# Rotating queries and keys in the projection, and making attention's first maxima key chunk by key chunk

## The reference, cut to what matters

```python
def apply_rope(x, cos, sin):
    half = x.shape[-1] // 2
    x1, x2 = x[..., :half], x[..., half:]
    return jnp.concatenate([x1 * cos - x2 * sin, x1 * sin + x2 * cos], axis=-1)

def diff_attend(q, k, v, lam):
    s = jnp.einsum('bqhmd,bkhmd->bhmqk', q, k) * (DA_QK ** -0.5)
    p = jax.nn.softmax(s, axis=-1)
    w = p[:, :, 0] - lam * p[:, :, 1]
    return jnp.einsum('bhqk,bkhv->bqhv', w, v)
```

## Time and profile before

| | us |
|---|---|
| median of 3 runs | 7244.72 (7240.84 to 7279.03) |
| the profiled execution | 7235.89 |
| its span | 7234.0 |
| PE busy | 5861.2 (81%) |
| DVE busy | 3119.6 (43%) |
| ACT busy | 1715.9 (24%) |
| POOL busy | 2013.9 (28%) |
| projections, by the trace | about 150 to 1250 and 3700 to 4960 |
| attentions start, by the trace | 2515.9 and 6082.9 |

### The profile page before, as it was taken

The page is one execution under the profiler, slowest core; times in us unless marked ns, Lnnn a source line. Parts: engine busy times, 40 slices in busy tenths (PEclk is TensorE's granted clock), DMA queues, the critical chain, the costliest instruction groups (busy, mean ns, idle before and its releaser), DMA issues. The chain is left out here.

```text
span 7234.0 us, 78073 instructions
## 1 busy us (share of the span) xinstructions
PE 5861.2 (81%) x27236; PEld 3103.1 (43%) x27272; DVE 3119.6 (43%) x5057; ACT 1715.9 (24%) x4089; POOL 2013.9 (28%) x1396
## 2 busy tenths in 40 slices
PE   4999999812688699998989999996218886999989
PEld 1444444411566533333434444443116664333334
DVE  0222222268566565551122333333875666555412
ACT  1111111100233324443011211211003332344421
POOL 0000000012333348887000000000223332688830
PEclk7999999855899889998999999997559997999989
DMA  7111111044322110001421111112433222000022
GB/s 257 49 45 45 47 46 44 31 134 130 107 79 79 54 34 7 7 5 41 192 91 49 45 47 46 47 40 63 126 117 104 79 86 64 1 7 7 4 83 92
DMA packets 294466, 475.52 MB, mean 66 GB/s; under 512 B 112612, under 2 KB 165172, under 8 KB 287268
## 3 DMA queue, kind: packets, MB, share of 16 engines
q1 hardware_dynamic: 262500, 383.00, 15.7%
q10 hardware_dynamic: 25632, 55.62, 2.1%
q0 software_dynamic: 6048, 33.11, 1.3%
HBM read 313.82 MB, written 157.51 MB: 65 GB/s over the span
## 5 line engine op out<-in xcount | busy, mean ns | idle before, releaser
L456 PE MATMUL psum<-group_W,projection_hT 128*128 128x512 f32 (+2 forms) x5040 | 2024.8, 559 | 52.5 <-DVE projection_hT L548 52.5
L456 PEld LDWEIGHTS psum<-group_W,projection_hT 128*128 128x128 f32 x5040 | 967.6, 193 | 1062.6 <-issue 1020.0
L1965 POOL TENSOR_TENSOR attention_SA<-attention_SA,attention_PT 128x1024 f32<-128x1024 f32 x512 | 1193.3, 2350 | 123.5 <-ACT attention_PT L2107 78.9
L2023 DVE TENSOR_REDUCE attention_mxp<-psum 128x1 f32<-128x512 f32 (+1 forms) x1016 | 653.6, 686 | 646.2 <-PE psum L2144 645.5
L2107 ACT ACTIVATE attention_PT<-psum 128x512 f32<-128x512 f32 (+1 forms) x1168 | 630.4, 592 | 888.1 <-PE psum L2193 859.4
L565 DVE TENSOR_SCALAR projection_e<-projection_e 128x256 f32<-128x256 f32 (+1 forms) x180 | 57.5, 319 | 1499.6 <-ACT projection_e L512 1499.6
L2144 PE MATMUL psum<-attention_QK 32*128 32x512 f32 (+1 forms) x2592 | 678.8, 642 | 10.3 <-DVE attention_mxp L2012 6.7
L2187 PE MATMUL psum<-attention_QK 32*128 32x512 f32 x2336 | 676.2, 656 | 0.0
L2205 PE MATMUL psum<-attention_PT,attention_va 128*64 128x512 f32 x2336 | 642.7, 630 | 0.0
L505 ACT ACTIVATE projection_ut<-psum 128x512 f32<-128x512 f32 (+1 forms) x360 | 149.9, 427 | 1696.8 <-PE psum L456 1696.8
L2318 PE MATMUL psum<-output_W,output_yT 128*128 128x512 f32 x1088 | 477.1, 597 | 20.4 <-DMA output_W<-in_w_out 20.4
(11 more groups left out here) (329 smaller groups left out, 7039.1 us busy)
## 6 DMA issues: line engine op xcount, KB each, us to landing
u<-projection_ut SPq DMA_DIRECT2D x252, 256.0 KB, 2.0
states_x<-xbc SPq DMA_DIRECT2D x108, 384.0 KB, 4.2
mixing_hg<-u SPq DMA_DIRECT2D x36, 1024.0 KB, 5.0
modulation_wm<-in_w_mod SPq DMA_DIRECT2D x12, 2048.0 KB, 8.7
group_W<-in_w_in SPq DMA_DIRECT2D x8, 2316.0 KB, 33.7
output_y<-y SPq DMA_DIRECT2D x34, 512.0 KB, 4.5
group_W<-in_w_in POOLq DMA_DIRECT2D x6, 2316.0 KB, 27.4
xbc<-projection_ut SPq DMA_DIRECT2D x36, 384.0 KB, 2.3
```

The lines of the kernel that those rows point to most:

```text
L456: ins = nc.tensor.matmul(ps[n % RING][:, 0:w], hT[b][:, q], W[q][:, c0:c0 + w], start=(q == 0), stop=(q == KT - 1))
L1965: G.tensor_tensor(SA[x % 2][:, rs, 0:w], one[:, rs, 0:w], PT[i % PTB][:, rs, 0:w], ALU.add) \
L2023: bk.release(V.tensor_reduce(mxp[x % 2][:, q:q + nn, 2 * pr + j, a], bk[job, j][:, 0:nn * (hi - lo)].rearrange("p (q n) -> p q n", q=nn), ...
```

## The change

The projection rotates the queries and keys itself. For block 3 ACT copies nothing any more; DVE multiplies the bank with the cosines and (half-swapped) with the sines, frees the bank, and writes the sum to `u`. The cosines and sines of the round's two tiles are loaded by SP at the start of each round (24 KB each), ahead of the round's stores. The counts of ACT's copies fall from 9 to 8 a tile.

Attention loads the rotated tiles and PE transposes them at once, into banks 4 and 5 (the prologue uses 0 to 3, 6 and 7); ACT copies as before. SP issues the small constants first, and loads a tile when the buffer's former tile is transposed. ACT makes the small exponential of `lm` ahead of its copies. The prologue's order becomes chunk, query tile, pair. PE turns six tiles (two of the context and the four of the first queries), two more before the first chunk, and ahead of each further chunk the tiles that the chunk after it needs (four, four, two), between the jobs of the maxima.

```diff
@@ projection
-             3: [(OFF["da_q"], 512, 1.0)], 4: [(OFF["da_v"], 256, 1.0)], 5: [(OFF["ss_xbc"], 512, 1.0)],
+             3: [], 4: [(OFF["da_v"], 256, 1.0)], 5: [(OFF["ss_xbc"], 512, 1.0)],
...
                 for r, kind, i in rounds(sp):
                     for b in range(2):
+                        sp.dma_start(rp[b][:].rearrange("p a f -> p (a f)"), k.rope[r * 2 + b]).then_inc(s[f"rope_in{b}"], 16)
+                    for b in range(2):
                         t = r * 2 + b
...
+                            if n == 3:
+                                hold(sp, s["rotated"], r * 2 + (b + 1), s["turns"])
...
                         for n, (c0, w) in enumerate(BLOCKS):
+                            if n == 3:
+                                continue
                             act.wait_ge(s["block_mm"], r * 20 + (b * 10 + n + 1))
...
+                            if n == 3:
+                                lo, w = BLOCKS[n]
+                                four = lambda a: a.rearrange("p (n x f) -> p n x f", x=2, f=16)
+                                cos = rp[b][:, 0].unsqueeze(1).unsqueeze(1).to_broadcast([P, w // 32, 2, 16])
+                                sin = rp[b][:, 1:3].unsqueeze(1).to_broadcast([P, w // 32, 2, 16])
+                                bank = ps[n % RING][:, lo - c0:lo - c0 + w]
+                                dve.wait_ge(s[f"rope_in{b}"], r * 16 + 16)
+                                dve.wait_ge(s["block_mm"], r * 20 + (b * 10 + n + 1))
+                                nc.vector.tensor_tensor(four(ra[:, 0:w]), four(bank), cos, ALU.mult)
+                                nc.vector.tensor_tensor(four(rb[:, 0:w]), skew(bank, 16, [[32, w // 32], [-16, 2], [1, 16]]), sin,
+                                                        ALU.mult).then_inc(s[f"bank_free{n % RING}"], 1)
+                                dve.wait_ge(s[f"bank_free{n % RING}"], r * 4 + (2 * b + 2))
+                                dve.wait_ge(s[f"st{n}"], (r * 2 + b) * 16 + 16)
+                                nc.vector.tensor_tensor(u[:, lo:lo + w], ra[:, 0:w], rb[:, 0:w], ALU.add).then_inc(s["rotated"], 1)
+                                dve.wait_ge(s["rotated"], r * 2 + (b + 1))
...
@@ attention
-    prologue = [(q, a, pr) for q in range(QG) for a in range(5) for pr in range(2)]
+    prologue = [(q, a, pr) for a in range(5) for q in range(QG) for pr in range(2)]
...
-                sp.dma_start(rp[:].rearrange("p t a f -> p t (a f)"), k.rope.rearrange("t p n -> p t n")).then_inc(s["rope_in"], 16)
...
+                for t in range(NT):
+                    b = t % 4
+                    if t >= 4:
+                        sp.wait_ge(s["key_mm"], t - 3)
+                    sp.dma_start(xb[b][:], k.u[t, :, OFF["da_q"]:OFF["da_q"] + 512]).then_inc(s[f"x_in{b}"], 16)
...
-                dve.wait_ge(s["rope_in"], 16)
-                f4 = lambda a: a.rearrange("p (n x f) -> p n x f", x=2, f=16)
-                for t in range(NT):
-                    b = t % 4
-                    dve.wait_ge(s[f"x_in{b}"], 16 * (t // 4 + 1))
-                    cos = rp[:, t, 0].unsqueeze(1).unsqueeze(1).to_broadcast([P, 16, 2, 16])
-                    sin = rp[:, t, 1:3].unsqueeze(1).to_broadcast([P, 16, 2, 16])
-                    V.tensor_tensor(f4(ra[t % 2][:]), f4(xb[b][:]), cos, ALU.mult)
-                    st.then(V.tensor_tensor(f4(rb[t % 2][:]), skew(xb[b][:], 16, [[32, 16], [-16, 2], [1, 16]]), sin, ALU.mult))
-                    if t >= 2:
-                        dve.wait_ge(s["key_mm"], t - 1)
-                    V.tensor_tensor(rot[t % 2][:], ra[t % 2][:], rb[t % 2][:], ALU.add).then_inc(s["rotated"], 1)
...
+                def keys(tiles):
+                    for t in tiles:
+                        pe.wait_ge(s[f"x_in{t % 4}"], 16 * (t // 4 + 1))
+                        if t >= 2:
+                            pe.wait_ge(s["key_copied"], t - 1)
+                        for a in range(4):
+                            ins = nc.tensor.transpose(k.bank[4 + t % 2][:, a * P:(a + 1) * P], xb[t % 4][:, a * P:(a + 1) * P], k.ident[:])
+                        ins.then_inc(s["key_mm"], 1)
...
-                pe.wait_ge(s["key_copied"], NT)
+                made = CT + QG
+                keys(range(made))
                 for n, (q, a, pr) in enumerate(prologue):
+                    if q == 0 and pr == 0:
+                        ahead = min(NT, groups[0][3][a][1] // P + 4)
+                        keys(range(made, ahead))
+                        made = max(made, ahead)
+                        pe.wait_ge(s["key_copied"], max(CT + QG, groups[0][3][a][1] // P))
```

More of the change, by code:

```diff
@@ L362, in projection @@
         small = [k.sb(c, f"small{b}", [P, 8]) for b in range(2)]
+        rp = [k.sb(c, f"rp{b}", [P, 3, 16]) for b in range(2)]
+        ra = k.sb(c, "ra", [P, 512])
+        rb = k.sb(c, "rb", [P, 512])
         G = k.sb(c, "G", [P, KT, 2])
@@ L411, in _ @@
                             if plain[n] and n != 8:
-                                hold(sp, s["copied"], r * 18 + (b * 9 + sum(bool(plain[m]) for m in range(n + 1))), s["turns"])
+                                hold(sp, s["copied"], r * 16 + (b * 8 + sum(bool(plain[m]) for m in range(n + 1))), s["turns"])
+                            if n == 3:
+                                hold(sp, s["rotated"], r * 2 + (b + 1), s["turns"])
                             if n in gated:
@@ L431, in _ @@
                     sp.wait_ge(s[n], 16 * (NT + 1))
+                for b in range(2):
+                    sp.wait_ge(s[f"rope_in{b}"], 8 * NT)
             @block.tensor
@@ L515, in _ @@
                             elif n != 8:
-                                act.wait_ge(s["copied"], r * 18 + (b * 9 + sum(bool(plain[m]) for m in range(n + 1))))
+                                act.wait_ge(s["copied"], r * 16 + (b * 8 + sum(bool(plain[m]) for m in range(n + 1))))
                                 act.sem_inc(s[f"bank_free{n % RING}"], 1)
                             if n == 8:
-                                act.wait_ge(s["copied"], r * 18 + (b * 9 + 8))
+                                act.wait_ge(s["copied"], r * 16 + (b * 8 + 7))
                                 act.sem_inc(s[f"bank_free{n % RING}"], 1)
@@ L2078, in _ @@
                 act.wait_ge(s["memsets"], 1)
+                act.wait_ge(s["lam_dot"], 1)
+                A(lm[:, 0:2], lm[:, 0:2], ACT.Exp).then_inc(s["lam_exp"], 1)
                 for t in range(NT):
                     act.wait_ge(s["key_mm"], t + 1)
-                    A(QK[:, :, t * P:(t + 1) * P], k.bank[t % 4][:].rearrange("p (a n) -> p a n", a=4), ACT.Copy) \
+                    A(QK[:, :, t * P:(t + 1) * P], k.bank[4 + t % 2][:].rearrange("p (a n) -> p a n", a=4), ACT.Copy) \
                         .then_inc(s["key_copied"], 1)
-                act.wait_ge(s["lam_dot"], 1)
-                A(lm[:, 0:2], lm[:, 0:2], ACT.Exp).then_inc(s["lam_exp"], 1)
                 def turned(x):
@@ L2129, in _ @@
                 T = nc.tensor.matmul
-                for t in range(NT):
-                    pe.wait_ge(s["rotated"], t + 1)
-                    if t >= 4:
-                        pe.wait_ge(s["key_copied"], t - 3)
-                    for a in range(4):
-                        ins = nc.tensor.transpose(k.bank[t % 4][:, a * P:(a + 1) * P], rot[t % 2][:, a * P:(a + 1) * P], k.ident[:])
-                    ins.then_inc(s["key_mm"], 1)
+                def keys(tiles):
[6 more added lines that the diff above has]
+                        ins.then_inc(s["key_mm"], 1)
                 rows = lambda r: slice(DQ * r, DQ * r + DQ)
```

15 lines of the change are left out of this document (3 added, 12 removed).

## The result

The changed kernel takes 7192.9 us (median of 5 runs, 7188.0 to 7209.4), the kernel before 7253.5 beside it (5 runs, 7240.8 to 7291.8). The ratio is 0.9892, 95% interval 0.9857 to 0.9928: 52 to 104 us faster. The forecast was 45 us, so faster is right, and the gain, 61 us between the medians and 78 by the ratio, came out above the stated range of 27 to 55. (The time 7192.9 by itself lies between 7186 and 7222, but that range hung on a kernel before at 7244.7, and beside the changed kernel it took 7253.5.) In two further measurements of the same kernel the ratio is 0.9942 and 0.9939. Over all runs made for this study (29 of the changed kernel, 124 of the one before, the experiment *null* included) the mean falls by 45.7 us, interval 33 to 58. The mean over many runs is thus near the forecast.

A forecast was written before the change was run, and what follows sets the result against it. PE bounds the projection, DVE the start of attention. Per layer 28.0 us earlier first product less 5.3 of waits is 22.7, 45.4 in all, projection nothing: 7199 us at the median's level; gain range 27 to 55, 7186 to 7222 once widened.

The forecast's parts named there:

- First tile: Start of attention: the first tile's load, issued at 2516.85 us, lands at 2520.2, with bounds of 2519.5 and 2521.0.
- Pitch of a tile: Start of attention: loaded tiles are transposed one every 1.1 us, with bounds of 0.96 and 1.93, the old pitch.
- First product: Start of attention: after eight turned tiles PE's first product comes 28.0 us earlier than before, bounds 28.9 and 22.2.
- Waits between the chunks: Attention's maxima: DVE waits for PE's inner transposes, 8.6 us a layer at 1.2 GHz, 2.0 at 2.4; 5.3 taken.
- a sign of being wrong: Attention's maxima: DVE idle over 10 us would mean that PE's transposes are dearer than thought.
- First read: Attention's maxima: DVE first reads 2.13 us after PE's first product, an estimated 1.3 at 2.4 GHz.
- rival 3: Attention: the wait moves to the gate's load, POOL late by some 6 us a layer; gain 33, 7212 us, chance 0.04.
- rival 4: Projection: DVE's three instructions at block 3 are exposed, up to 76 us against 45; +31, 7275 us, chance 0.05.
- The sign given for it: Projection: if the forecast is right, PE's busy share stays as before and DVE's idle time falls by 74 us.
- rival 1: Start of attention: loads or a low clock bind, pitch nearer the old one; gain 27 to 36, 7213 us, chance 0.15.
- rival 2: Start of attention: the clock rises and stays, waits of 2.0 us a layer; gain 52, 7193 us, chance 0.10.
- Numbers: Whole kernel: 7190.5 us from the profiled execution, 7199 at the median's level; range widened by 4 us each side.

The follow-up runs named there:

- null: The kernel before timed once more against itself, nothing changed: 7254.5 us (12 runs), ratio 1.001.
- triple: Changed kernel with six more of the rotation's first product on DVE for each tile in the projection: 7211.5 us (10 runs), ratio 0.9928 to the kernel before.
- spread: Changed kernel with PE turning one tile after every second job of the maxima, not blocks before chunks: 7226.8 us (12 runs), ratio 0.9943 to the kernel before.
- again: The changed kernel timed and profiled once more, nothing altered: 7207.9 us (12 runs), ratio 0.9942 to the kernel before.
- proj_only: Changed projection with the attention of before, so queries and keys are rotated twice: 7271.5 us (10 runs), ratio 1.002 to the kernel before.
- fill: Kernel of spread with a bfloat16 product, later overwritten, ahead of each score in the last half of attention: 7566.1 us (6 runs), ratio 1.0402 to the kernel before.

## Why the prediction was right or wrong

**First tile.** The forecast was 4.3 us from the stage's start to its landing; its transposes start at 5.3. The issue is where it was expected, and the landing was slow: 2.6, 3.3 and 4.9 us at least, in the median and at most (2.6, 2.7 and 4.2 before). From issue to use it was 4.4 us for the first tile, against 4.0 before, with the table's load no longer ahead of it. That was the case which the rule of the Trainium skill ("DMA: Bandwidth & Descriptors", Specifications) on transfers under 512 B had priced at 1.2 us better. No such gain is seen; but another load with short rows (`gr`, 256 B a row) stood ahead, so the rule isn't refuted.

**Pitch of a tile.** Forecast 1.1. Seven tiles in 2524.66 - 2517.41 = 7.25 us are 1.04, between PE's 0.96 and the 1.05 of the bytes.

**First product.** Forecast 13.1 us after the stage's start, measured 2525.24 - 2512.14 = 13.10; 28.0 earlier than before, as forecast; over the eight profiled stages of the changed kernel and of *triple* it is 12.8 to 13.4. In the first of them two errors cancel: the landing 1 us late, the pitch and the last transposes (0.66 us, at 2.4 GHz, not 1.12) 0.9 early.

**Waits between the chunks.** Right in place and mechanism, low in size. The forecast for 1.2 GHz was 3.5, 3.5 and 1.6; measured 4.50, 4.50 and 2.68 (11.7 against 8.6). For 2.4 GHz it was 1.0, 1.0 and none; measured 1.38, 1.38 and 2.46, the last of them at a clock that had fallen again, as in the prologue of the earlier trace rows. Over the eight stages the sum is 7.5 us, not the 5.3 taken. *spread* shows that it is all PE's transposes. In three of the eight DVE is idle for over 10 us, which the prediction had named as a sign of being wrong, and for the reason that it gave there: the transposes cost more than thought. The Trainium skill ("TensorE: Matmul & The Clock Gate", HAM oscillation) says that pauses of PE let its clock fall; in three of the eight stages the sum was that of the low clock (11.7 or 11.8), in the others 4.5 to 5.2, so neither level can be counted on. The fall under the column sums came without such a pause: PE was busy, by the profile, for all 2.70 us ahead of it in *again*.

**First read.** Against that, DVE reads 1.2 us after the first product in five of the eight stages, not 2.13 (the clock is 1.00 there in the first layer's stage above); in the three others it is 2.1. The narrow reads at the end keep their pace. Together the prologue is 63.9 us in the mean over eight stages, forecast 63.6, and the gain 22.4 a layer, forecast 22.7: 45 us in all.

**Gate's load (rival 3).** POOL has it multiplied at 2559.62 + 4.76 = 2564.4, nine us ahead of the maxima's end at 2573.5, where 5 were forecast. Out.

**Projection (rival 4).** Nothing exposed, by PE's busy time, by the lengths of the projections and by *triple*. Out. The sign given for it was misjudged, though: DVE's idle time ahead of the gates fell by 213 us and not by 74, because 138 us of it moved ahead of the rotation. Rivals 1 and 2, the low clock through and the high clock through, are each what some of the stages did, at 11.7 and about 5 us of waits; the pitch near the old 1.93 that rival 1 feared was not seen (1.04). That rival 2's time, 7193, is the measured median is chance: its 2.0 us of waits were seen in no stage.

**The whole.** The mechanism held, and each term of the prologue's sum to a microsecond or two. What failed is the step "Numbers". It took the spread of the result from the distance between lowest run and median, 4 us, and the prediction has no term and no row for the end of the attention stages: it puts that at nothing without a reason. The runs showed there a step of 37 us (first layer) or 54 us (second) in some executions. Of the three runs shown ahead of the prediction one was at 7279, 38 us above the lowest, most likely that step.

How this made the first result can be read from the single runs. All five of the changed kernel were in its lowest group, which with 20 of 29 in that group happens in one case of six; two of the five of before, 7279 and 7292, were in an upper one. The means of the five differ by 66.8 us: 51 between the runs of the lowest groups, and 16 from those two. Drawing five runs of each kernel at random from all those measured gives a difference of means between 22 and 68 us in eight draws of ten, 9 and 79 in 95 of 100. A range of 27 to 55 with 4 on each side was too narrow for that.

The nearness of the mean over many runs (45.7 us) to the sum (45.4) is in part luck as well. Between executions of the lowest groups the change gains 51.5 us, 6 more than the prologues give. The upper groups lie higher over the lowest with the change, so that they add some 21 us to its mean and 15 to that of before, which takes the 6 away again.

**What stays open.** The profiled executions give only part of the gain. The first and second attention stage take 904 and 889 us in the mean of before and *null*, 888 and 872 in the mean of those stages of the changed kernel and of *triple* (whose attention is the same) that have no low tail. That is 33 us, where the prologues alone give 45. The profiled execution of before (7235.9) lies below all of the 124 runs, and the one of after (7209.4) is the highest of its five, so the pair of profiles understates the gain. The main loop behind the prologue gives back some 7 and 3 us: 825 instead of 818 in layer 1, 806 instead of 803 in layer 2. But *proj_only*, with the attention of before, has 824 and 809 there as well. So these few profiles can't show that the change costs the main loop anything, and no experiment took this apart. Nor is it shown where the 51.5 us between the lowest groups come from beyond the prologues' 45. Open too is why the clock of the tail stays down when it falls at one moment of the column sums and not when at another, and what sets that moment.

## What to carry to other kernels

Where an engine that only prepares stands between loads and first products, moving its work to a stage where it idles pays by the whole pitch it set, and *triple* is the cheap way to see how much room that stage has. When a second producer is fed in blocks between the jobs of a pipeline, set it singly: here the block of four transposes cost 1.4 to 4.5 us each time, and one after every second job nothing. Before giving a range, look whether the runs shown fall into groups, and find the stage that makes the step; a sum good to a microsecond does not give the median of five if a step of 37 to 54 us comes in a third of the runs. And read the clock in windows short enough to name the instruction under which it falls: windows of 40 us can't tell the column sums from the end of the maxima, 32 us earlier.

## What the runs showed of the hardware

PE's granted clock can stay at 1.2 GHz for 126 us while PE is busy, by the profile, for all of them (*again*, 6840.8 to 6967.1; 94 to 108 records in 40 us instead of 177). In another execution of the same kernel it came back from the same fall after 13.7 us. In every traced attention stage the fall came 1.4 to 5.1 us into a block of 16 one-column products, and with other products of PE beside what followed it was over within 11 us. A full-array product between two 32-row ones costs their overlap: one takes 2.07 us then, where two took 2.08, and *fill* as a whole was 339 us slower than *spread*. Loads of the same 256 KB tile land 2.7 us after their issue in the median when a slower consumer paces them, and 3.3 when they follow each other at 1.04 us. DVE's first read of a pair of products came 1.2 us after they started at a granted clock of 1.00, and 2.1 at 0.56.
